# Storing a unit's gated activations from ScalarE's queue during the next unit, in place of SyncE's queue at the unit's end

## What is computed

```python
h2 = _rmsnorm(x, g_ffn) * (1 + sc2) + sh2
g = h2 @ f_w_gate
u = h2 @ f_w_up
gconv, new_fconv = _causal_dwconv(g, f_conv, f_conv_w, f_conv_b)
x = x + gt2 * ((jax.nn.silu(gconv) * u) @ f_w_down)
...
y_prompt = _rmsnorm(xp, g_final)
```

## Time and profile before

| | before |
|---|---|
| three runs | 2910.37, 2912.29, 2895.03 us, median 2910.37 |
| the profiled execution | 2913.92 us; its span 2912.1 us |
| TensorE busy (matmuls) | 2715.7 us, 93% of the span |
| VectorE busy | 1491.8 us, 51% |
| ScalarE busy | 1119.3 us, 38% |
| mean granted TensorE clock | 0.967 |
| data moved | 531.44 MB, mean 182 GB/s |

### The profile page before, as it was taken

How to read it: one execution, slowest core, us unless ns; L and a number is a source line. 1 busy time by engine, 2 the same in 40 slices (tenths; PEclk the granted TensorE clock), 3 DMA queues, 4 the chain that set the end, 5 groups by cost and what they waited for, 6 DMA issues and landing times.

```text
span 2912.1 us, 42652 instructions
## 1 busy us (share of the span) xinstructions
PE 2715.7 (93%) x15479; PEld 2397.6 (82%) x15479; DVE 1491.8 (51%) x2851; ACT 1119.3 (38%) x1949; POOL 253.3 (9%) x412
## 2 busy tenths in 40 slices
PE   4999999999769999997999998999999999899998
PEld 2888888999646777776899987889999778899887
DVE  2533334242346666664877755545444554544446
ACT  1332324332323454544444444433333443333344
POOL 0000000000033333330000000000000000000000
PEclk8999999999779999998999999999999999999999
DMA  9343334222555444434877755667776666787656
GB/s 321 135 152 125 123 111 142 89 68 75 166 178 176 143 131 136 131 116 122 276 241 240 243 187 183 217 198 247 222 222 193 205 215 198 243 257 249 226 179 220
DMA packets 355270, 531.44 MB, mean 182 GB/s; under 512 B 28084, under 2 KB 253510, under 8 KB 354930
## 3 DMA queue, kind: packets, MB, share of 16 engines
q1 hardware_dynamic: 348836, 522.61, 54.3%
q10 hardware_dynamic: 6288, 6.88, 0.8%
HBM read 390.88 MB, written 140.75 MB: 183 GB/s over the span
## 4 chain that ended last, share of the span: by engine, by line
PE 41%; DVE 4%; DMA 3%; ACT 2%; issue 2%; SPq 0%; DVEq 0%; ACTq 0%; POOL 0%; POOLq 0%
PE acc_ps L3354 12%; PE acc_ps L3324 9%; PE acc_ps L3325 9%; PE acc_ps L3326 9%; DMA f_raw_g<-in_f_w_down 2%; PE acc_ps L3365 2%; DVE f_conv L3752 1%; ACT f_w_hi L3523 1%; DMA f_w_lo<-scratch_sums 1%; ACT f_conv L3495 1%; DVE f_h_lo L3898 0%; DVE f_w_lo L3774 0%; DVE f_h_lo L3807 0%; ACT f_gate_on L3506 0%; ACT f_part L3464 0%
## 5 line engine op out<-in xcount | busy, mean ns | idle before, releaser
L3324 PE MATMUL acc_ps<-f_h_hi,f_w_hi 128*128 128x384 f32 (+1 forms) x1848 | 615.2, 333 | 40.2 <-ACT f_part L3464 25.7
L3326 PE MATMUL acc_ps<-f_h_hi,f_w_lo 128*128 128x384 f32 (+1 forms) x1848 | 609.9, 330 | 0.0
L3325 PE MATMUL acc_ps<-f_h_lo,f_w_hi 128*128 128x384 f32 (+1 forms) x1848 | 608.7, 329 | 0.0
L3324 PEld LDWEIGHTS acc_ps<-f_h_hi,f_w_hi 128*128 128x128 f32 x1848 | 352.0, 190 | 48.5 <-issue 34.0
L3325 PEld LDWEIGHTS acc_ps<-f_h_lo,f_w_hi 128*128 128x128 f32 x1848 | 351.3, 190 | 0.1
L3326 PEld LDWEIGHTS acc_ps<-f_h_hi,f_w_lo 128*128 128x128 f32 x1848 | 351.0, 190 | 0.0
L3769 DVE TENSOR_TENSOR f_w_lo<-f_raw_g,f_w_hi 128x1024 fp32r<-128x1024 f32 x110 | 134.7, 1225 | 215.2 <-ACT f_w_hi L3523 214.7
L3354 PE MATMUL acc_ps<-f_w_hi 128*128 128x512 f32 x660 | 208.9, 398 | 27.5 <-DVE f_w_lo L3774 27.5
L3523 ACT ACTIVATE f_w_hi<-f_raw_g 128x1024 fp32r<-128x1024 f32 x110 | 116.6, 1060 | 257.4 <-PE acc_ps L3354 212.2
L959 PE MATMUL p_unit<-w_in_hi,p_ht_hi 128*128 128x512 f32 (+1 forms) x544 | 205.9, 378 | 9.8 <-DVE p_ht_lo L698 7.5
L3354 PE MATMUL acc_ps<-f_w_hi,f_w_lo 128*128 128x512 f32 x660 | 206.8, 395 | 0.0
(11 more groups left out here) (570 smaller groups left out, 4875.6 us busy)
## 6 DMA issues: line engine op xcount, KB each, us to landing
f_raw_g<-in_f_w_down SPq DMA_DIRECT2D x120, 512.0 KB, 3.4
f_w_hi<-scratch_sums SPq DMA_DIRECT2D x88, 512.0 KB, 4.3
f_w_lo<-scratch_sums SPq DMA_DIRECT2D x88, 512.0 KB, 5.4
f_raw_g<-in_f_w_gate SPq DMA_DIRECT2D x66, 512.0 KB, 4.2
scratch_sums<-f_w_hi SPq DMA_DIRECT2D x44, 512.0 KB, 2.7
scratch_sums<-f_w_lo SPq DMA_DIRECT2D x44, 512.0 KB, 3.5
f_mid_raw<-scratch_mid SPq DMA_DIRECT2D x110, 192.0 KB, 3.3
scratch_mid<-f_mid SPq DMA_DIRECT2D x44, 384.0 KB, 2.6
```

Of the source, the lines that this page charges most:

```text
L3324: t.matmul(dst, hi, h_hi[:, op, k, 0:w], start=(opening and k == 0), stop=False, skip_group_check=True)
L3325: t.matmul(dst, hi, h_lo[:, op, k, 0:w], start=False, stop=False, skip_group_check=True)
L3326: last = t.matmul(dst, lo, h_hi[:, op, k, 0:w], start=False, stop=(k == 3), skip_group_check=True)
```

## The change

The store of a unit's gated activations leaves SyncE's queue. ScalarE issues it, one unit later: in unit n, when the convolution of unit n is done and before the SiLU of unit n, it stores the activations of unit n-1. The first unit of a span (written out, f = 0) stores nothing at that place; the last unit of a span stores the one before at that place and its own at the unit's end, after the high part of the mid rows of down step 1. The transfer, its buffers and its semaphores are the same.

```diff
--- before.py
+++ after.py
@@ SyncE @@
-            def store_mid(s, q, j):
-                f = q * 2 + j
-                w, t0 = spans[s][2], spans[s][0]
-                sp.wait_ge(s_mid, f + (s * KF + 1))
-                dst = S["mid"][:, f, t0:t0 + w] if isinstance(f, int) else (
-                    S["mid"][:, bass.ds(f, 1), t0:t0 + w].rearrange("p o t -> p (o t)"))
-                sp.dma_start(dst, mid[j][:, 0:w]).then_inc(s_mst[j], 16)
...
-                store_mid(s, q, j)
@@ ScalarE @@
+            def store_mid(s, n, f, j):
+
+                w, t0 = spans[s][2], spans[s][0]
+                dst = S["mid"][:, f, t0:t0 + w] if isinstance(f, int) else (
+                    S["mid"][:, bass.ds(f, 1), t0:t0 + w].rearrange("p o t -> p (o t)"))
+                act.wait_ge(s_mid, n + 1)
+                act.dma_start(dst, mid[j][:, 0:w]).then_inc(s_mst[j], 16)
...
                 act.wait_ge(s_conv, n + 1)
                 if not very_first:
                     act.wait_ge(s_mid, n)
+                if not (static and f == 0):
+                    store_mid(s, n - 1, f - 1, 1 - j)
                 width = spans[s][2]
                 a_.activation(gate_on[:, 0:width], conv[:, 0:width], ACT.Silu).then_inc(s_on, 1)
...
                     keep_mid(s, 0, 0, 1)
+                    store_mid(s, n, f, j)
```

## The result

The changed kernel took 2913.38 us in the median of 14 runs (2904.09 to 2921.7), the kernel before 2905.01 us in the median of 14 (2895.03 to 2912.29): ratio 1.0027, 95% interval 1.0014 to 1.004. It is slower by some 8 us, 0.3%. The profiled execution of the changed kernel took 2907.16 us (span 2905.4 us), less than that of before, whose 2913.92 us lies above all 14 of these runs; single executions differ by more than the effect, so the two profiles are read place by place and not by their spans.

The account below looks back on a forecast made before the run. TensorE was taken as the bound, through its standstills in the feed-forward stage. Price 20.8 us less gains 14.1 us gave +6.7 us, so 2917.1 us beside the median of 2910.37 us; range 2894 to 2936 us.

Parts of the forecast that it names:

- The price on the circle: Store issue delays the loop third product, sixth product, convolution, SiLU, copy, next third product; 20.8 us with all spans and entries.
- The second span's room: Slack of 0.69 us before TensorE's third product in the second span; a 0.60 us loop issue fits in free.
- units with squares: Second span's three units already waiting for squares of the previous span's rows pay 3 x 0.42 = 1.3 us.
- the failed gain: Rival: load leaves earlier but the third down step stays late; only the cost remains, 2931 to 2934 us; chance 0.13.
- The gain: Third down step of each span: stalls behind SyncE's in-order wait go, 10.2 us, plus clock drops; 14.1 us in all.
- The entries: Entry to the down projection in each span: TensorE's wait on the last SiLU's piece grows, 3 x 0.42 = 1.3 us.
- The upper end of the sum: With issue prices of 0.98 and 1.16 us over all spans and entries: +39.1 us, or 2949.5 us.
- the five cases: Chances: own forecast 0.63, the failed gain 0.13, The hidden issue 0.12, The issue that only moves 0.06, The dear issue 0.06.
- The issue that only moves: Rival: 22.7 us of issuing passes from SyncE to ScalarE, neither being the bound; 2910 us; chance 0.06.
- The dear issue: Rival: ScalarE's issue takes 0.91 us, so stalls grow in all three spans; 2949.5 us; chance 0.06.
- The hidden issue: Rival: ScalarE's store issue ahead of the SiLU costs nothing, leaving only the gains; 2896 us; chance 0.12, wholly or mostly.

Follow-up runs that it names:

- e3: Changed kernel with SyncE again waiting for the last unit's gated product in each span, stores still on ScalarE: 2926.42 us, ratio 1.0083 to before.
- e1: Changed kernel with ScalarE's store issued ahead of its wait for the convolution instead of behind it: 2890.93 us, ratio 0.9947 to before.
- e8: Changed kernel run again unaltered for a second profile: 2921.55 us.
- e5: Kernel before, run again unaltered for a second profile: stalls at the third down step 8.7 us in sum; no total time given.
- e4: Changed kernel with each store cut into two halves of the columns, issued one behind the other: 2954.01 us, ratio 1.0177 to before.
- e2: Kernel before, stores still on SyncE, with the loads of down step 2 ahead of each span's last-unit store: 2889.28 us, ratio 0.9941.
- e6: Changed kernel with the store issued right behind the SiLU instead of ahead of it: 2894.21 us, ratio 0.9965 to before.
- e7: Changed kernel with the store issued earlier, behind the high part of the next gate weights: 2889.8 us, ratio 0.9943 to before.

## Why the prediction was right

The forecast was +6.7 us, the measured difference +8.4 us between the medians, and 1.0027 x 2905 gives +7.8 us. By its steps:

**The price on the circle.** The sum said 20.8 us. e3 measured it at 20 to 24 us and the step from e1 to the changed kernel at 23 us. The third span was to take 10.9 us and took 11.5 to 11.8 in the two profiles of the changed kernel and 10 in e3's (292.3 us). A loop unit was to pay 0.60 us and paid 0.54 (13.30 against 12.76 us between SiLUs); one written out 0.42 us, and paid 0.39. The first span was to take 7.3 us. Its loop units paid 0.25 to 0.35 us each; with the others that is 5 to 6 us (from the SiLU of unit 1 to that of unit 21 before's two profiles took 294.5 us, after, e8 and e3 took 299.6 to 300.2). In the profile of after only five of them show as waits of TensorE, since a gap of 0.2 us is hardly told from the spacing of the matmuls:

```profile
1582.06 0.41 PE L3315 MATMUL acc_ps<-f_h_hi,f_w_hi 128*128 128x384 f32 x1 [0.20 <-ACT f_part L3463]
...
1597.06 0.41 PE L3315 MATMUL acc_ps<-f_h_hi,f_w_hi 128*128 128x384 f32 x1 [0.19 <-ACT f_part L3463]
```

These are two third products in a row, 15.00 us apart where a unit was 14.75. Counting waits, I forecast some 44 on this copy; the profile lists 30 and e8's 35, for that reason. Lengths of units are the better measure.

**The second span's room.** The step said 0.69 us and no price in the loop. That room came from an execution whose units in that span took 14.76 us. They don't always. Below, the SiLU of two units in the profile of before, and of two in e5:

```profile
2106.34 0.85 ACT L3506 ACTIVATE f_gate_on<-f_conv 128x768 f32<-128x768 f32 x1 [1.18 <-DVE f_conv L3752]
...
2121.10 0.85 ACT L3506 ACTIVATE f_gate_on<-f_conv 128x768 f32<-128x768 f32 x1 [1.20 <-DVE f_conv L3752]
```

```profile
2102.67 0.85 ACT L3506 ACTIVATE f_gate_on<-f_conv 128x768 f32<-128x768 f32 x1 [1.20 <-DVE f_conv L3752]
...
2117.26 0.85 ACT L3506 ACTIVATE f_gate_on<-f_conv 128x768 f32<-128x768 f32 x1 [1.23 <-DVE f_conv L3752]
```

14.76 and 14.59 us for the same code. With the shorter unit the room is about 0.5 us (an estimate: 0.69 less the 0.19 by which the unit is shorter), and a delay of 0.53 us just fills it: the units after are 14.6 to 14.8 us long. Where the room is full, each of 17 units pays some 0.1 us. That is a term of up to 2 us which the sum had at zero. The three units with squares were to pay 0.42 us each, and their waits grew from 7.5 to 8.6 us, 0.37 each.

**The clock in the units with squares.** Their waits are not all that they cost. The third of them in the second span, from SiLU to SiLU, in the windows view of before and then of after:

```profile
1985.69:2003.12 17.43, 14.98 (x86) 14.69 (x85) 9.05 (x14) 6.06 (x10) 0.73 (x2) 1.00 0.78 254
```

```profile
1977.21:1997.77 20.56, 17.72 (x86) 17.43 (x86) 9.05 (x14) 6.06 (x11) 0.73 (x2) 0.83 0.67 212
```

The unit is 3.1 us longer, and nearly all of it is the granted clock, 0.83 for 1.00, behind a standstill of TensorE that was 0.4 us longer. Units with squares came with a clock of 1.00, 0.90 to 0.91 or 0.82 to 0.83, and from one to the next they are some 1.2 to 1.6 us longer. Over the six of them (three each in the second and third span) the clock took 13.8, 10.5, 8.8 and 12.2 us in the four profiles with the issue ahead of the SiLU (after, e8, e3, e4), and 6.8 to 10.3 us in the six others: 11.3 against 7.7 us in the mean. The two groups overlap, so that the longer standstill brings more drops is likely and not shown. My sum had nothing for it; the 3 us that I named for such drops stood with the rival of the failed gain alone. With the 3.6 us between the two means the sum's 20.8 us comes to 24, the upper end of what was measured.

**The gain.** The sum said 14.1 us; e2 measured 17 us, e1 15 us, e3 12 to 16 us. The mechanism is shown by e2 and e3: the one load behind one wait, in three places. My size of it rests on one profile. The first stall was 5.08 us there, 4.12 in e5 and 2.96 in e3. The clock drops that I priced at 3.9 us came to 5.2 and 5.4 us over the longer windows. Stalls and drops together are 10.2 + 5.2 = 15.4 us in the profile of before, 8.7 + 5.4 = 14.1 us in e5 and 13.3 us in e3, beside the 12 to 17 us of the runs. That the 14.1 us of the sum is the difference of the down stretches to the tenth is chance: its first stall was too long and its clock drops too short. The last down stretch, where things scatter least, shows it best: a stall of 2.28 to 2.46 us and 1.8 us of clock are 4.1 to 4.3 us, and the stretch is 4.2 us shorter.

**The entries.** The second step's wait went from 0.21 to 0.60 us in the first span, 0.39 us for the 0.42 forecast (0.4 us in each of the other two spans as well). ScalarE's own wait for the last product (1.02 us of idle time, some 0.5 expected) had no price, as forecast: the split still ended before TensorE was through with the step before.

**How much of the hit was luck.** The mechanism and the signs of both halves are confirmed. That the net came out within 2 us is partly luck: the price was up to 3 us larger than the sum had it, and the gain by e1 and e2 1 to 3 us larger, so the two misses offset, and each is as large as their difference. Within the price, a first span and a loop unit that I had too dear stand against the clock and the second span's full room, which I had at nothing. The upper end of the sum has a slip: with an issue of 0.91 us the first span costs 14 x 0.98 + 6 x 0.80 = 18.5 us, not 17.8, which makes that end 2950 us. And the chances of the five cases already add up to 1.00, so the 0.02 for what I had missed has no place among them.

**The rivals.** The failed gain is refuted by the third step in the profile after, which has no stall, and by e3, where the stalls come back. The issue that only moves is refuted by e2: one load's place in the queue was worth 17 us with the stores where they had been. The dear issue is refuted by the rows: 338 to 356 ns in all 66. The hidden issue was the closest to a truth that I had put aside: it doesn't hide where it was placed, since ScalarE was idle there, but e6 shows that it does, for the most part, behind an activation that has been handed over. Of the Trainium skill's rule that issuing from several engines only saves the sequencer's issue time ("DMA: Bandwidth & Descriptors", section "Issuing engines are not separate DMA queues"), the runs show both sides: e2 says that the second queue was not needed for the gain, and e3 that an in-order wait, which the rule doesn't speak of, was worth 12 to 16 us.

## What to carry to other kernels

When a transfer moves to a compute engine's queue, ask what that engine does at the moment of issue. Ahead of a step that others wait for and on an idle engine, the issue is paid in full, 0.39 us here and 0.54 us with an address from registers, times the units; a few lines higher it was free, beside an earlier split (e1) or in idle time that something else ended (e7). And before a whole stream of transfers leaves a queue, look for the one transfer that its wait holds up: here three pairs of loads carried the whole gain, and moving them alone gave it without the price.

## What the runs showed that I had not expected

- The same units of the second span took 14.75 us in some executions and 14.56 us in others at full granted clock, over the 17 units from the fifth to the one before the last, with no wait of TensorE in the list. The difference, some 3 us in this span, is over a third of the effect that was measured here. What sets it I don't know.
- Half of a store costs no less to issue than a whole one: 338 to 1280 ns with a median of 362 over the 132 halves, against 338 to 356 with a median of 338 over the 66 wholes. Two in a row took 0.82 to 1.10 us (one pair 1.66), and delayed the SiLU by 0.54 us more than one in the unit shown. The number of issues counts here, not the bytes.
- An issue behind a running activation was mostly free (e6: ratio 0.9965, against 1.0027 with the issue ahead of that activation).
